# An MLP of 4096 hidden features: from eight block products in three row groups to seven block products in two halves through DRAM

## The reference, cut to what matters

```python
D_MODEL = 1024; SEQ = 2048; DEC_BATCH = 8; DEC_SEQ = 8; D_FF = 4096; EPS = 1e-6
def rms_norm(x, g):
    y = x * lax.rsqrt(jnp.mean(x * x, axis=-1, keepdims=True) + EPS)
    return y * g
def sqrelu_mlp(h, w_up, w_down):
    u = jnp.einsum('btd,df->btf', h, w_up)
    return jnp.einsum('btf,fd->btd', jnp.square(jax.nn.relu(u)), w_down)
...
hp = hp + a_p                  # a_p: attention and mLSTM heads through w_out (the output projection)
hp = hp + sqrelu_mlp(rms_norm(hp, norm2_g[l]), w_up[l], w_down[l])     # the same for hs, 64 rows
y_prompt = rms_norm(hp, norm_f_g)
```

## Time and profile before

| | us |
|---|---|
| time, median of 3 runs (lowest, highest) | 2979.95 (2974.84, 2980.64) |
| span of the profiled execution | 2977.5 |
| PE busy in it | 2862.7 (96%) |
| DVE, ACT, POOL busy | 1429.0, 926.1, 1001.3 |
| first matmul of the MLP, start of its last one | 1477.70, 2963.96 |

### The profile page before, as it was taken

One profiled execution on the slowest core, in us unless ns is written; L12 is line 12 of the kernel. 1 busy time (PEld: TensorE's weight loads), 2 busy tenths in 40 slices (PEclk: granted clock), 3 DMA queues, 4 the chain that ended last, 5 costly groups with the idle time before them and its releaser, 6 DMA issues.

```text
span 2977.5 us, 47544 instructions
## 1 busy us (share of the span) xinstructions
PE 2862.7 (96%) x18291; PEld 2482.8 (83%) x18291; DVE 1429.0 (48%) x3364; ACT 926.1 (31%) x1740; POOL 1001.3 (34%) x589
## 2 busy tenths in 40 slices
PE   7999999999999978999999999999999999999998
PEld 5878788887778757678899999989999998899997
DVE  5522555334788855676343333344333333544444
ACT  4301322112677742431122222243222222422222
POOL 1212012211445530210154343444434344545443
PEclk8999999999999988999999999999999999999999
DMA  4322223335364558945452322235222323533332
GB/s 137 113 103 95 99 95 121 107 111 156 121 204 144 163 179 324 392 150 186 147 197 97 123 94 108 97 120 226 94 108 96 125 94 117 208 126 134 139 127 84
DMA packets 124714, 421.28 MB, mean 141 GB/s; under 512 B 18639, under 2 KB 44371, under 8 KB 104838
## 3 DMA queue, kind: packets, MB, share of 16 engines
q1 hardware_dynamic: 104124, 367.71, 34.9%
q10 hardware_dynamic: 19290, 47.37, 4.1%
q0 software_dynamic: 1152, 4.19, 0.4%
HBM read 350.70 MB, written 135.63 MB: 163 GB/s over the span
## 4 chain that ended last, share of the span: by engine, by line
PE 47%; DVE 1%; DMA 1%; ACT 1%; POOL 0%; issue 0%; ACTq 0%; DVEq 0%
PE bank L220 15%; PE bank L222 15%; PE bank L221 15%; PE bank L236 0%; PE bank L235 0%; DMA mlp_acc<-x 0%; POOL mlp_wu_lo L2724 0%; DVE mlp_acc L2954 0%; DVE mlp_acc L2989 0%; DMA mlp_xb<-x 0%; PE bank L3099 0%; DVE mlp_xn L2942 0%; POOL mlp_xb L2766 0%; ACT mlp_wu_hi L2782 0%; DMA out_y_prompt<-mlp_acc 0%
## 5 line engine op out<-in xcount | busy, mean ns | idle before, releaser
L2954 DVE TENSOR_TENSOR mlp_acc<-mlp_acc,bank 128x512 f32<-128x512 f32 x542 | 348.2, 684 | 364.0 <-PE bank L222 355.6
L220 PE MATMUL bank<-mlp_hT_hi,mlp_wu_hi 128*128 128x384 f32 (+1 forms) x1536 | 496.6, 323 | 3.1 <-PEq L3243 3.1
L222 PE MATMUL bank<-mlp_hT_hi,mlp_wu_lo 128*128 128x384 f32 (+1 forms) x1536 | 495.4, 323 | 0.0
L221 PE MATMUL bank<-mlp_hT_lo,mlp_wu_hi 128*128 128x384 f32 (+1 forms) x1536 | 495.1, 322 | 0.0
L2942 DVE TENSOR_TENSOR mlp_xn<-mlp_xn 128x384 f32<-128x384 f32 (+1 forms) x192 | 204.6, 1071 | 510.4 <-ACT mlp_xn L2800 491.2
L220 PE MATMUL bank<-mlp_wd_hi,mlp_u_hi 128*128 128x512 f32 x1024 | 399.9, 391 | 5.0 <-DVE mlp_acc L2954 4.9
L221 PE MATMUL bank<-mlp_wd_lo,mlp_u_hi 128*128 128x512 f32 x1024 | 398.9, 390 | 0.0
L222 PE MATMUL bank<-mlp_wd_hi,mlp_u_lo 128*128 128x512 f32 x1024 | 398.8, 389 | 0.0
L2728 POOL TENSOR_TENSOR mlp_wd_lo<-mlp_wd_raw,mlp_wd_hi 128x2048 fp32r<-128x2048 f32 x48 | 222.0, 4625 | 391.6 <-ACT mlp_wd_hi L2788 391.6
L2737 POOL TENSOR_TENSOR mlp_u_lo<-mlp_xn,mlp_u_hi 128x384 fp32r<-128x384 f32 (+1 forms) x192 | 177.8, 937 | 360.5 <-ACT mlp_u_hi L2809 360.5
L220 PEld LDWEIGHTS bank<-mlp_hT_hi,mlp_wu_hi 128*128 128x128 f32 x1536 | 288.8, 188 | 5.2 <-issue 3.5
(11 more groups left out here) (377 smaller groups left out, 4702.7 us busy)
## 6 DMA issues: line engine op xcount, KB each, us to landing
mlp_wu_raw<-in_w_up SPq DMA_DIRECT2D x48, 1024.0 KB, 4.8
mlp_wd_raw<-in_w_down SPq DMA_DIRECT2D x48, 1024.0 KB
out_win_k_sample<-in_cache_k SPq DMA_DIRECT2D x48, 680.0 KB, 6.3
out_win_v_sample<-in_cache_v SPq DMA_DIRECT2D x48, 680.0 KB, 7.2
p_w_raw<-in_w_tok SPq DMA_DIRECT2D x10, 2048.0 KB
sm_vin<-in_cache_v SPq DMA_DIRECT2D x8, 2048.0 KB, 13.4
proj<-p_stage ACTq DMA_DIRECT2D x53, 256.0 KB, 2.0
parts<-mx_part SPq DMA_DIRECT2D x48, 264.0 KB, 3.6
```

Source lines behind the costliest of these rows:

```text
L220: nc.tensor.matmul(out, ah, bh, start=(k == 0), stop=False)
L221: nc.tensor.matmul(out, ah, bl, start=False, stop=False)
L222: ins = nc.tensor.matmul(out, al, bh, start=False, stop=(k == n - 1))
L2954: ins = v.tensor_tensor(acc[:, t, 512 * e:512 * e + 512], acc[:, t, 512 * e:512 * e + 512], bank[4 + 2 * (i % 2) + e][:], ALU.add)
```

## The change

Both GEMMs of the MLP are cut into 2x2 blocks, and each 2x2 product is formed by seven block products of sums of blocks in place of eight products of blocks (Strassen's scheme in the form with few additions). `h` (rows) is cut into two halves of its width 1024 and into pairs of row sets; `w_up` and `w_down` are cut likewise. Rows are handled in two halves: `g = 0` are tiles 0 to 7, `g = 1` are tiles 8 to 15 and the 64 sample rows (`NH = 544` columns for each of its two row sets).

- `project_out`: all 17 tiles get their norm here (`HEAD = NP + 1`). The transposed result goes through `hs` to the DRAM tensor `hT`; the first half is loaded back at tile 11 as four blocks, and DVE makes the other three slots (`h_sum`) at tiles 12 to 15.
- `mlp`, up: 16 sets for `g = 0` with 512 columns, then 32 sets (two column pieces `q` for each of 16 chunks of weights) with 272 columns. A set is seven products of 12 matmuls (`chain_products`, L2638 to L2640 of the changed kernel), the last three of them added into banks that already hold a product. Between products 4 and 5, 5 and 6, 6 and 7 DVE or ACT must have read the bank (`first`, `up_post`). The four results of a set are squared and go to the DRAM tensor `u`. The weights of `w_up` are summed on DVE (`sum_up`), rounded on ACT and subtracted on DVE.
- `w_down` is prepared in the up part: 32 units (`load_unit`, `unit_sums`, `unit_hi`, `unit_low`, `store_unit`) turn 512 KB of `w_down` each into seven summed and split blocks in the DRAM tensor `wd`. There is one buffer for a unit, and `unit_sets` says in which set each is worked on: sets 0 to 14, then 20, 22, ..., 44 and 21, 23, 25, 27.
- between the halves (set 15) the second half of `hT` is loaded, and DVE and POOL make its sums, each for one column piece.
- `mlp`, down: for each half eight blocks `kb` of 512 hidden features, in each four pairs of tiles (`steps`), one pair a step of seven products with six matmuls of 512 columns; for `g = 1` also a step of 16 matmuls for the sample rows. For a step four blocks of `u` are loaded (`load_u(m)`, three buffers), POOL makes their sums (`sums`), ACT rounds, DVE subtracts (`u_low`). For each `kb` both parts of `wd` are loaded (`load_down`, 2 x 3.67 MB, two buffers). DVE adds the seven results to `acc` (`down_post`).
- 72 of the 96 cache copies move to `project` (`copies`), 24 stay, in sets 20 to 43.

The core of the diff (lines of before start with -, of the changed kernel with +):

```diff
-            for g in range(G):
...
-                up(g, FB * g, 0)
-                up(g, FB * g + 1, 1)
-                down(g, 0, 0)
+        for s in range(S0):
+            g, c, q = sets[s]
+            ci = NC * g + c
+            at, n = piece(s)
+            w = ci % 2
+            for i in range(7):
+                if q == 0:
+                    pe.wait_ge(wu_lo_ready, 3 * ci + PART[i] + 1)
+                if c == 0:
+                    pe.wait_ge(h_lo_ready, (0 if g == 0 else 7 * (1 + q)) + max(ORDER[g, q].index(k) for k in range(i + 1)) + 1)
+                if i < 4:
+                    if s >= 2 and i == 0:
+                        pe.wait_ge(relued, 4 * (s - 2) + 2)
+                    elif s >= 2:
+                        pe.wait_ge(post, 5 * (s - 2) + (1, 4, 5)[i - 1])
+                elif i == 4:
+                    pe.wait_ge(first_copied, s + 1)
+                else:
+                    pe.wait_ge(post, 5 * s + (2, 3)[i - 5])
+                chain_products(nc, bank[4 * (s % 2) + CHAIN[i]][:, 0:n],
+                               [(wu_hi[w][:, i, P * k:P * (k + 1)], wu_lo[w][:, i, P * k:P * (k + 1)],
+                                 h_hi[:, i, k, at:at + n], h_lo[:, i, k, at:at + n]) for k in range(4)], i < 4, mm)
...
+        def load_unit(w):
+            kb, j, e = unit_of(w)
+            if w:
+                sp.wait_ge(un_out, 32 * w)
+            sp.dma_start(un_raw[:, 0:7:2], K.ins["w_down"][kb, j, e].rearrange("p (a c) -> p a c", a=4)).then_inc(un_in, 16)
+        def store_unit(w):
+            kb, j, e = unit_of(w)
+            sp.wait_ge(un_lo_ready, w + 1)
+            for hl, src in enumerate((un_hi, un_lo)):
+                dst = K.wd[kb, hl].rearrange("p (a j c) -> p a j c", a=7, j=2)[:, :, j, 256 * e:256 * e + 256]
+                sp.dma_start(dst, src[:].bitcast(F32)).then_inc(un_out, 16)
...
+        for st in steps:
+            if st.p is not None and st.m + 2 < M_END:
+                if st.m:
+                    sp.wait_ge(mm, mm_end(pair[st.m - 1]))
+                load_u(st.m + 2)
+            if st is first_of[st.kbi] and st.kbi + 1 < 16:
+                if st.n:
+                    sp.wait_ge(mm, mm_end(steps[st.n - 1]))
+                load_down(st.kbi + 1)
...
+            down_post(st, 0)
+            down_post(st, 1)
...
+            if st.m + 1 < M_END:
+                u_low(st.m + 1, 0)
+            down_post(st, 2)
+            down_post(st, 3)
+            if st.m + 1 < M_END:
+                u_low(st.m + 1, 1)
+            down_post(st, 4)
```

More of the change, by code:

```diff
@@ L346, in load_tile, with copies @@
                 sp.dma_start(staged[:, x], rows).then_inc(staged_in, 16)
+            def copies(i, ev):
+                for e in range(6):
+                    sp.wait_ge(tok_mm, ev + e)
+                    for name in "kv":
+                        K.copy_cache(sp, name, i, e)
             for g in range(2):
@@ new lines, in mlp @@
+    M = K.to_mlp
+    NH = M.NH
+    HALF = (4 * P, NH)
+    COL0 = (0, 8 * P)
+    NC = DFF // 256
+    UNITS = 32
+    place = K.place
+    sets = [(0, c, 0) for c in range(NC)] + [(1, c, q) for c in range(NC) for q in range(2)]
+    S0 = len(sets)
+    LAST = S0 - 1
+    unit_sets = sorted(list(range(15)) + [16 + 2 * c for c in range(2, 15)] + [17 + 2 * c for c in range(2, 6)])
+    unit_at = {s: w for w, s in enumerate(unit_sets)}
+    assert len(unit_sets) == UNITS
+    bank = K.bank
+    h_hi, h_lo, h_raw = M.h_hi, M.h_lo, M.h_raw
@@ new lines, in mlp @@
+    f_sum, f_ssq, f_var, f_root, f_newton, f_gained = (sem("mlp_f_" + n) for n in ("sum", "ssq", "var", "root", "newton", "gained"))
+    y_ready, y_last = sem("mlp_y_ready"), sem("mlp_y_last")
+    y_out = [sem(f"mlp_y_out{p}") for p in range(5)]
+    class Step:
+        pass
+    steps = []
+    for g in range(2):
+        for kb in range(8):
+            for p in ([None] if g else []) + list(range(4)):
+                st = Step()
+                st.g, st.kb, st.p, st.kbi, st.n = g, kb, p, 8 * g + kb, len(steps)
+                st.m = (8 * g + kb) * 4 + p if p is not None else None
+                st.mm0 = steps[-1].mm0 + (3 if steps[-1].p is None else 7) if steps else 7 * S0
+                st.po0 = steps[-1].po0 + (3 if steps[-1].p is None else 7) if steps else 0
+                steps.append(st)
@@ new lines, in mlp, with nth, mm_end, last_read @@
+    N = len(steps)
+    ends = steps[-1].mm0 + 7
+    pair = {st.m: st for st in steps if st.p is not None}
+    first_of = {st.kbi: st for st in reversed(steps)}
+    samp = {st.kbi: st for st in steps if st.p is None}
+    M_END = 64
+    def nth(F):
+        return 4 if F is None else F + (F >= 4)
+    def mm_end(st):
+        return st.mm0 + (3 if st.p is None else 7)
+    def last_read(st, b):
+        if st.p is None:
+            return st.po0 + {X_: 3, W_: 2}.get(b, 0)
+        return st.po0 + {X_: 5, Y_: 2, Z_: 6, W_: 7}[b]
```

1257 lines of the change are left out of this document (724 added, 533 removed).

## The result

The changed kernel takes **3216.77 us** (median of 4 runs, 3214.16 to 3224.80) against 2977.39 (4 runs, 2974.12 to 2980.64) for the old kernel: 1.0806 times as long, 95% interval 1.0788 to 1.0825, 239 us more. The forecast was 3038 with 2920 to 3105 as its range. Slower was right, the size was not.

A forecast was written before the change was run, and what follows sets the result against it. The prediction took PE, busy 96% of the span, as the bound. Its terms, -209 us for the matmuls and the rest added costs, summed to +58 on the 2977.5 us span, plus 2.4 to the median: 3038 us, range 2920 to 3105.

The forecast's parts named there:

- The matmuls: Whole MLP: fewer products at the paces of 512 and 272 columns take 1277 us against 1486, -209.
- The copies in `project`: Cache copies moved to `project`: cost nothing, as stores have 5 us of slack; up to 15 us if stores are pushed past.
- The norms in `project_out`: `project_out`: the 88 norm transposes that leave the MLP return here for 11 tiles, +9 us.
- Units in consecutive sets: Up part, sets 20 to 28: a unit's round of 17.9 us exceeds a set of 10.4, +60, bounds 20 and 75.
- Units in every other set: Up part, second half, units in alternate sets: the forecast had no cost here, 0.
- Between the halves: Around sets 15 to 17: DVE's and POOL's SBUF work exclude each other, set 16 starts late, +28, bounds 8 and 36.
- Up to down: Start of the down part: PE waits for loads behind weights and `acc`, 5, 7 and 9 us, +21, bounds 8 and 30.
- The blocks of the down part: Down part: `u` loads land late behind each block's 7.34 MB of weights, +101 (35 in half 0, 66 in half 1).
- Small loads not held up: Down part: `u` lands within 14 us of the block's start, the 101 us go, 2937 us; chance 0.17.
- Unit round hidden: Up part: the units' stores land early, the 60 us of consecutive sets go, 2978 us; chance 0.08.
- PE stays the bound: MLP: PE stays the bound and all else is covered, 2808 us; chance 0.06.
- Exclusion in every down step: Down part: POOL's sums delay DVE's `u_low` by some 1.5 us in all 64 steps, 96 us, 3134 us; chance 0.12.

The follow-up runs named there:

- e4: Changed kernel without the 72 cache copies in `project`, so those cache rows are not written: 3191.94 us.
- e11: Changed kernel with the edits of e2, e6 and e3, the `project` copies moved into the MLP, and the order changed at five places: 2991.67 us.
- e12: Changed kernel with the edits of e2, e6, e3, the order of e11, 60 copies kept in `project`, 12 moved to down steps: 2945.11 us.
- e6: Changed kernel with only the table of unit sets changed, to sets 0 to 17 and each odd set 19 to 45: 3128.50 us.
- e7: Changed kernel with the unit's load issued near the end of the set before, where that set holds no unit: 3186.96 us.
- e8: Changed kernel with POOL's four sums between the halves waiting until DVE has made its four: 3211.43 us.
- e3: Changed kernel with POOL's wait for the final norm's gain moved from ahead of the third pair's sums to its first use: 3210.58 us.
- e2: Changed kernel with each block's 7.34 MB of down weights cut into four parts in SP's queue, one behind each step's `u` load: 3084.22 us.
- e1: Changed kernel with the loads of the prepared down weights moved from SP's queue to ACT's: 3266.38 us.
- e5: As e1, but the weights go in 14 DMAs of 1024 columns, with rows of 4 KB: 3156.62 us.

## Why the prediction was wrong, step by step

The trace is 176 us above the forecast. 78 of them are waits that the forecast held at nothing: the unit's load in every other set (45), the copies in `project` (26) and the burst of h loads (7). 65 are waits whose mechanism it had, but too short: blocks of the down part (27), consecutive units (24), between the halves (14). 17 are a wait of another cause than forecast (up to down), 11 the pace of the matmuls.

- **The matmuls** (-209): right but for 11 us. The 272 columns took 0.1256 us, forecast 0.1242; the 512 columns of half 0 19.5 / 84 = 0.232 in place of 0.2267, which the down part keeps (9.51 / 42). Each matmul has its own weight load in both parts (PE and PEld both x17331), so that is not the difference; what is stays open.
- **Start of the MLP** (+20): 20.0, with some luck: the chain ahead of it cost 15.5 (forecast 12), set 0 only 4.5 (forecast 8).
- **The copies in `project`** (0, up to 15): the first failed step. I set the 5 us of slack of its stores against one pair of copies and called the rest free. In the trace the pairs follow each other every 5 us, four copies come within 2.2 us near 504, and twelve (8 MB) within 7.5 us near 593 and again near 638, there ahead of the gate tables. 26 us, shown by e4.
- **The norms in `project_out`** (+9): the norms themselves cost that, 8; the burst of four h loads at tile 11 cost 7 more, which no term held. With the loads spread (e11, e12) it is gone.
- **Units in consecutive sets** (+60, bounds 20 and 75): the mechanism was right, the size over the upper bound: 84. The round was 18.1 to 23.2 us, not 17.9. I had the stores land in 6.6 us and the load in 3.8 as if alone; but copies, `u` stores and raw weights are in the same queue. In sets 21 to 29 the trace has 7.0 to 11.1 us from a unit's first store to the next load, and 4.5 to 5.5 for the load. And I had no term for what PE loses behind each of the pauses, one to two products at the lower clock.
- **Units in every other set** (0): the step that failed worst, +45. I had looked only at the wait for the stores of the unit before; the load behind a copy and 1 MB, in the same list of SP that the diff section shows, was not costed. e6 took both away, e7 one half.
- **Between the halves** (+28, bounds to 36): 42. The exclusion was as forecast (set 16 begins 44.5 us after set 15, forecast 35), and e8 shows it by the durations; what was missing is that ACT's rounding of h, put ahead of the last up weights, waited 5.3 us for h and held DVE for 7.5.
- **Up to down** (+21): 38. The forecast blamed the third load for standing behind `acc`. It was POOL's wait for the gain, which stands in POOL's list ahead of the third sums: a wait I had not followed. e3 shows both: with that wait moved, the second and third steps are 6.5 and 13.9 us too long, where the forecast had +7 and +9 for loads behind the weights.
- **The blocks of the down part** (+101): 127.5, the mechanism exactly: one pause a block, in the third step of half 0 and the second of half 1, 7 and 11 us where 5.1 and 9.5 were forecast. e2 shows it. My remark that the 101 us would be gone if the transfers were shared out was wrong for two queues: e1 shared them, by packets and not by bytes, and it got worse.
- **Final norms** (+20) and the end (+3): 23.8 and 7.6.
- **The rivals.** Small loads not held up: refuted by e2. Unit round hidden: only in half 0. PE stays the bound: no. Exclusion in every down step: refuted by e2, where steps of 9.5 us hold both. Only the last of them was slower than the forecast, and by another cause; the case that came, most waits of the forecast longer and 78 us of waits that it held at nothing, was in no rival. The +-58 (the half widths as stated give 61) took the errors of the terms as independent. They were not: one cause, the length and the order of SP's queue, made most of them larger at once.

What stays open: `project` lost 18 to 32 us in runs with the same code there, and I did not find what sets it within that.

## What to carry to other kernels

A load is as late as everything issued ahead of it in its queue: for each wait write down the queue's contents at the issue, bytes and all, also for the sets and steps without a special event, and cut large prefetches into parts that stand behind the urgent small loads. When many engines hand on one result, list each wait of each engine's list ahead of it; e3 moved one and met the next. A scheme with fewer products pays only once its transfers are spread evenly: here the same work and bytes took 3217 us in one order and 2945 in another.

## What the runs showed of the hardware that was not expected

- Two queues share the transfer engines by packets: 132 packets of `u` to 130 of weights in e1, 957 to 941 in e5. `u` in packets of 0.5 KB got nothing to speak of beside weights in packets of 25.5 KB (22 us for 0.5 MB), and with 4 KB rows e5 was 110 us faster. In one queue, behind the same 7.34 MB, it took the same 22 us.
- Beside a sum on POOL, DVE sums and subtractions of 4 x 272 columns with all operands in SBUF took 3.45 to 3.59 us in place of 1.28, the length of POOL's (3.05 to 3.54) and not twice DVE's own.
- Behind each of the 32 longest pauses of the changed kernel's MLP (3.6 to 24.9 us) PE ran some 5 to 25 matmuls at half clock. With those behind shorter pauses it is 72 us over the MLP, a fifth of its loss.
